# A two-model transformer kernel on one core: norm parts made with the residual, linears placed inside attentions, a position table stored from all partitions

## The reference

```python
def first_block(...):                     # DEPTH = 2
    for l in range(DEPTH):
        h = rms_norm(x, norm_mix[l])
        x = x + (even_mixer if l % 2 == 0 else odd_mixer)(h, ...)
        x = x + memory_cross_attention(rms_norm(x, norm_cross[l]), rms_norm(mem, norm_mem[l]), ...)
        x = x + conv_ffn(rms_norm(x, norm_ffn[l]), ffn_w_up[l], ...)
def second_block(...):
    for l in range(DEPTH):
        x = x + HALF_STEP * swiglu(rms_norm_2(x, ffn1_norm[l]), ...)
        x = x + hybrid_mixer(rms_norm_2(x, mix_norm[l]), positions, ...)
        x = x + memory_cross_attention_2(rms_norm_2(x, ca_norm[l]), rms_norm_2(mem, mem_norm[l]), ...)
        x = x + HALF_STEP * swiglu(rms_norm_2(x, ffn2_norm[l]), ...)
    return rms_norm_2(x, final_norm)
```

## Time and profile before

| | |
|---|---|
| median of 3 runs | 2695.26 us (2693.7 to 2696.86) |
| the profiled execution's own time | 2693.7 us |
| its span, first to last instruction | 2693.7 us |
| PE busy | 2426.5 us, 90% |
| weight loads busy | 2237.8 us, 83% |
| DVE busy | 1680.1 us, 62% |
| ACT busy | 1115.9 us, 41% |
| mean granted TensorE clock | 0.918 of 2.4 GHz |
| HBM read | 357.78 MB, 135 GB/s over the span |

### The profile page before, as it was taken

One profiled execution on the slowest core, in us unless ns is written; L12 is line 12 of the kernel. 1 busy time (PEld: TensorE's weight loads), 2 busy tenths in 40 slices (PEclk: granted clock), 3 DMA queues, 4 the chain that ended last, 5 costly groups with the idle time before them and its releaser, 6 DMA issues.

```text
span 2693.7 us, 40616 instructions
## 1 busy us (share of the span) xinstructions
PE 2426.5 (90%) x17557; PEld 2237.8 (83%) x17557; DVE 1680.1 (62%) x2336; ACT 1115.9 (41%) x1314; POOL 31.5 (1%) x53
## 2 busy tenths in 40 slices
PE   6877899997688998999998789999999998789998
PEld 6747799994578998999984578999999994578997
DVE  4465587755467877666446767666666445767664
ACT  4334454433355444334342354334334253345332
POOL 0103000000000000000000000000000000000000
PEclk8878999997799999999996789999999997789998
DMA  7525245450124554555540234554555640043552
GB/s 217 142 26 143 94 158 187 158 189 16 63 94 143 188 188 141 188 181 156 158 136 1 68 126 140 186 176 164 179 188 158 168 149 16 28 160 109 179 188 79
DMA packets 322821, 365.40 MB, mean 136 GB/s; under 512 B 24495, under 2 KB 298691, under 8 KB 322515
## 3 DMA queue, kind: packets, MB, share of 16 engines
q1 hardware_dynamic: 316723, 349.12, 39.8%
q0 software_dynamic: 4336, 7.31, 1.7%
q10 hardware_dynamic: 1584, 6.36, 0.6%
HBM read 357.78 MB, written 4.98 MB: 135 GB/s over the span
## 4 chain that ended last, share of the span: by engine, by line
PE 76%; DVE 14%; ACT 8%; issue 2%; DVEq 0%; DMA 0%; ACTq 0%; PEldq 0%
PE bank L630 22%; PE bank L633 21%; PE bank L631 21%; DVE wlo L1223 3%; PE bank L781 2%; PE bank L828 2%; ACT xs_hi L989 2%; DVE wk L1296 2%; ACT whi L937 2%; PE bank L717 1%; PE bank L817 1%; ACT wk L991 1%; PE bank L705 1%; PE bank L783 1%; PE bank L725 1%
## 5 line engine op out<-in xcount | busy, mean ns | idle before, releaser
L630 PE MATMUL bank<-xs_hi,wlo 128*128 128x256 f32 x3920 | 1013.5, 293 | 94.9 <-DVE xs_lo L1293 42.8
L631 PE MATMUL bank<-xs_lo,whi 128*128 128x256 f32 x3920 | 994.8, 289 | 0.0
L937 ACT ACTIVATE whi<-raw 128x2048 fp32r<-128x2048 f32 (+2 forms) x344 | 638.7, 1860 | 836.9 <-PE bank L633 814.5
L1223 DVE TENSOR_TENSOR wlo<-raw,whi 128x2048 fp32r<-128x2048 f32 (+2 forms) x344 | 761.5, 2224 | 237.9 <-ACT whi L937 237.7
L630 PEld LDWEIGHTS bank<-xs_hi,wlo 128*128 128x128 f32 x3920 | 771.3, 197 | 116.6 <-issue 94.9
L631 PEld LDWEIGHTS bank<-xs_lo,whi 128*128 128x128 f32 x3920 | 775.9, 198 | 0.3
L633 PE MATMUL bank<-xs_hi,whi 128*128 128x256 f32 (+1 forms) x3920 | 572.3, 287 | 0.0
L633 PEld LDWEIGHTS bank<-xs_hi,whi 128*128 128x128 f32 (+1 forms) x3920 | 520.9, 196 | 4.3
L630 PE MATMUL bank<-act_hi,wlo 128*128 128x256 f32 x1056 | 276.4, 283 | 5.4 <-DVE wlo L1223 5.4
L631 PE MATMUL bank<-act_lo,whi 128*128 128x256 f32 x1056 | 276.3, 283 | 0.0
L633 PE MATMUL bank<-act_hi,whi 128*128 128x256 f32 x1056 | 212.9, 283 | 0.0
(11 more groups left out here) (205 smaller groups left out, 2057.9 us busy)
## 6 DMA issues: line engine op xcount, KB each, us to landing
raw<-in_ffn_w_gu SPq DMA_DIRECT2D x88, 1024.0 KB, 5.1
...
```

The lines of the kernel that those rows point to most:

```text
L630: eng.matmul(out, a[1], b[0], start=first and i == 0, stop=False, skip_group_check=True)
L631: eng.matmul(out, a[0], b[1], start=False, stop=False, skip_group_check=True)
L937: eng.activation(whi[i % SETS][:, 0:ch["n"]], raw[i % SLOTS][:, 0:ch["n"]], ACT.Copy).then_inc(S["weights_hi"], 1)
L1223: eng.tensor_tensor(wlo[i % SETS][:, 0:n], raw[i % SLOTS][:, 0:n], whi[i % SETS][:, 0:n].bitcast(F32), ALU.subtract)\
```

## The change

1. **Norm parts with the residual.** A linear or `ffn` that adds to `xT` now takes `then`, the next norm. As soon as a pair of tiles of `xT` is added, ACT makes its two `hi` tiles and its squares (`norm_pair`), DVE its two `lo` tiles (`norm_lo`). The parts go to one of two buffers `X`. The squares of a pair are summed by PE with two fp32 matmuls (`sum_pair`), 8 for a norm; the reduction on DVE is gone.
2. **No barrier to the next linear.** A stage with `join=True` has no drain and no wait; normed linears and `ffn` are such. Their first two units run in lockstep, pair by pair of tiles as these come (`as_it_comes`). Linears after a `split` take the parts tile by tile in the same way; the `split` stage is gone. Other stages keep the barrier.
3. **Linears inside attentions.** `enroll` puts units in a list, and `fill={slot: (emit, evacuate)}` of a `heads`, `index` or `attention` stage says at which step PE emits them and ACT and DVE split and evacuate. Moved: 8 units of the even mixer's input, 6 of the odd mixer's, the value units of all four cross attentions (2 each), the 12 gate units of each hybrid mixer, and the first half (4 half units of 24 matmuls each) of the output projections of the even and the odd mixer. Attention now has two score banks instead of four, and its own output banks; mLSTM and differential attention have one bank for transposes and one for outputs.
4. **Gates.** The tanh is done later (`flush`), often at the end of an attention; the scale by 0.5 is folded into what follows.
5. **Memory.** Both memories are transposed and normed once (in two stages of linears and at the end of one `heads` stage), stored to DRAM as four tensors `mem_in`, and loaded as a chunk by each cross attention. Its units are evacuated by ACT ("plain").
6. **Start and tables.** Gains of the first norm and chunk 0 are loaded first; x is normed at once, and memory, tables and parameters are handled after the first two units. POOL waits for no stage: `rpb` and `na_skew` go first. The T5 table is made as `t5_rows`, the same row on all 128 partitions, and stored in four DMAs of 512 KB.

```diff
-            def norm_input(nm):
-                for k in range(KT):
-                    eng.activation(xs[0][:, k, :], nm["src"][:, k, :], ACT.Identity, scale=cols[:, nm["gain"] + k:nm["gain"] + k + 1], bias=C("zero"))\
-                       .then_inc(S["xs_hi"], 1)
-                eng.activation(square, nm["src"][:, :, :], ACT.Square).then_inc(S["sq_ready"], 1)
+            def norm_pair(nm, p):
+                signal, value = nm["pairs"][p]
+                eng.wait_ge(S[signal], value)
+                two = xT[:, 2 * p:2 * p + 2, :]
...
+                for k in (2 * p, 2 * p + 1):
+                    eng.activation(X[nm["buf"]][0][:, k, :], xT[:, k, :], ACT.Identity, scale=cols[:, nm["gain"] + k:nm["gain"] + k + 1],
+                                   bias=C("zero")).then_inc(S["xs_hi"], 1)
+                if p < 3:
+                    eng.activation(squares[p].rearrange("p (k c) -> p k c", c=SEQ), two, ACT.Square).then_inc(S["sq_ready"], 1)
...
-            def enter(i):
-                if i:
-                    eng.wait_ge(S["act_stage"], i)
-                    eng.wait_ge(S["dve_stage"], i)
+            def enter(i, st):
+                if i and not st["join"]:
+                    eng.drain().then_inc(S["pe_stage"], 1)
+                    if st.get("after"):
+                        eng.wait_ge(S["att_done"], st["after"])
+                    fill(st, "pre")
+                    eng.wait_ge(S["act_stage"], st["bar"])
+                    eng.wait_ge(S["dve_stage"], st["bar"])
...
+            def sum_pair(nm, p):
+                eng.wait_ge(S["sq_ready"], 4 * nm["n"] + p + 1)
+                for i in range(2):
+                    m = eng.matmul(post_bank[1][:, 0:SEQ], C("add128"), squares[p][:, i * SEQ:(i + 1) * SEQ],
+                                   start=p == 0 and i == 0, stop=p == 3 and i == 1, skip_group_check=True)
...
+            def unit(u):
+                un = units_of[u]
+                emitted[0] = u + 1
+                arrived(un["chunk"])
+                bank_free(u)
+                for o, operands in un["mms"]:
+                    m = product(lin_bank[u % 2][:, o], operands, True, True)
+                m.then_inc(S["lin_ready"], 1)
+
+            def fill(st, slot):
+                if slot in st["fill"]:
+                    while emitted[0] < st["fill"][slot][0]:
+                        unit(emitted[0])
...
                 for i in range(len(units) + lag + 1):
                     if i < len(units):
                         scores(i)
+                    fill(st, i)
                     if 0 <= i - lag < len(units):
                         turn(i - lag)
...
+            def fill(st, slot):
+                if slot in st["fill"]:
+                    emit_end, evac_end = st["fill"][slot]
+                    split_upto(units_of[emit_end - 1]["chunk"] + 2)
+                    evac_upto(evac_end)
...
+            attention("softmax", [small_head(o, 0, 9, h, h * HD, h, bias=C3("causal"), row=h, top_k=True, causal=True) for h in range(6)],
+                      fill={0: (G[4], G[3]), 2: (G[5], G[4]), 4: (G[6], G[5]), 6: (G[7], G[6])}, tanh=G[5])
...
-            eng.dma_start(t5_skew.ap(), t5_vec.unsqueeze(1).to_broadcast([4, SEQ, 512])).then_inc(S["t5_stored"], 16)
+            for h in range(4):
+                eng.wait_ge(S["t5_rows_made"], h + 1)
+                eng.dma_start(t5_skew.ap()[h].rearrange("(p n) c -> p n c", n=2), t5_rows[:, h, :].unsqueeze(1).to_broadcast([P, 2, 512]))\
+                   .then_inc(S["t5_stored"], 16)
+            spill(0)
```

1121 lines of the change are left out of this document (691 added, 430 removed).

## The result

The changed kernel takes **2628.0 us** (median; 2626.3 to 2628.3) beside 2695.0 us before: a ratio of 0.9753, 95% interval 0.9738 to 0.9769. One more execution of it took 7835.6 us; it is left out of these figures, and no record says what it waited for. It is faster by 67 us, where 248 us were forecast, and lies 53 us above the upper end of the range. The profiled execution took 2627.7 us with a span of 2625.9.

A forecast was written before the change was run, and what follows sets the result against it. PE bounds the feed-forward layers; hand-offs between engines and the half clock bound heads and attentions. 2693.7 less 156 (linears inside attentions) less 93 (joints, start) gives 2445, with 1.6 to the median 2447 us; range 2345 to 2575.

The forecast's parts named there:

- the factor of 1.165: Heads and attentions with moved units: time over PE's 566 us of full-clock work, giving 659 us and a 156 us gain.
- a rival of its own in the prediction: Filled attentions keep a clock near 0.73, so PE needs 775 us there: 2561 us in all, chance 0.08.
- PE and DVE take turns at being late: Filled attentions, unit between scores and transposes (place 1): alternating lateness, priced within 1.165, giving 659 us.
- slower than before: Every filled unit: splits issued only after the head's waits, 9.95 us a unit, 2801 us in all, chance 0.03.
- DVE as the smaller engine: Heads and attentions with moved units: DVE holds 438 us against PE's 566, so PE is the larger.
- Joints: Outside the filled attentions: feed-forward layers, cross attentions' linears, outputs, hybrids, inputs, branches and start together save 93 us.
- the hybrid split and output leave 26: Hybrid split and output: 33.8 us falls to 26 with parts tile by tile, saving 16 us for two.
- Three pairs of products before it needs the last: Feed-forward layer's end: PE has 8.3 us of work before needing the last pair, about 3 us late; 1 us left.
- Start: Kernel's start: first product at about 17 us instead of 31.2, yet 1 us lost overall; bounds 10 gained, 10 lost.
- Table store: Position table stored from 128 partitions: some 25 us from about 45, in time for the even mixer, worth nothing.
- Its rival's price, 66 us: Store still takes 95.6 us, so an evacuation stalls the even mixer some 66 us: 2511 us, chance 0.03.
- The two rules: Throttled clock is the default and activity releases it; ScalarE and VectorE queues are in-order. Both weighed for filled attentions.

The follow-up runs named there:

- e10: Changed kernel with units inside heads, index and attentions running 6 of their 48 matmuls, results wrong: 2523.8 us, ratio 0.9364.
- e11: Changed kernel with only 64 of 2048 columns copied and subtracted for units inside heads, index and attentions, all matmuls kept: 2570.6 us, ratio 0.9539.
- e3: Changed kernel with VectorE adding a finished unit to the residual before splitting the chunk after the next, in linears making norm parts: 2619.8 us, ratio 0.9730.
- e2: Changed kernel with barriers back at all 18 stages that joined the one ahead, norm parts still made with the residual: 2707.8 us, ratio 1.0058.
- e9: Changed kernel with each of the four position-table rows stored from 4 partitions in place of 128: 2682.2 us, ratio 0.9965.
- e13: Changed kernel with ScalarE, in attentions, copying the next chunk's weights ahead of its copy of the turned probabilities: 2612.5 us, ratio 0.9700.
- e16: Changed kernel with four thrown-away matmuls ahead of the wait for probabilities in 52 attention slots without a unit: 2645.9 us, ratio 0.9819.
- e17: Thrown-away matmuls added to the changed kernel with half units, add ahead of split, other slots and early weight copy together: 2622.0 us, ratio 0.9731.

## Why the prediction was wrong

- **Direction and kind: right.** Faster, with the attentions as the place of the largest gain.
- **The step that failed is the factor of 1.165** on TensorE's 566 us "in full-clock time". It took the filled stages as running at full clock and put all loss into idle time, 93 us. Measured: 560 us of full-clock work (6 less than forecast), 125 us idle (32 more) and 89 us of half clock (forecast 0). 32 + 89 - 6 = 115 us, the miss in these stages. On the forecast's 566 us the factor should have been 774.4/566 = 1.37. Its source mixed two measures: 37.9/34.31 = 1.10 is length over busy time at a clock of .55, while the factor was put on full-clock time, by which that stage is 37.9/(34.31 x 0.55) = 2.0. The clock was a rival of its own in the prediction, with a chance of .08 and a clock of .73 for all of it; in truth both held at once, the clock at .81 to .87 in the odd and hybrid mixers, and engines that wait in turn. The reason against that rival, that units in linears run at full clock, did not carry over: after 6.8 us without a matmul at the start of the sparse attention, the first unit ran at half clock for most of its length (granted clock at half from 2196.7 to 2206.9), its matmuls 0.21 us apart and then 0.12:

```profile
2200.24 1.61 PE L968 MATMUL bank<-ft 64*128 64x128 f32 x4 [6.78 <-DVEq L1480]
...
2204.94 0.41 PE L727 MATMUL bank<-x_hi,wlo 128*128 128x256 f32 x1
2205.15 0.41 PE L728 MATMUL bank<-x_lo,whi 128*128 128x256 f32 x1
...
2207.01 0.28 PE L727 MATMUL bank<-x_hi,wlo 128*128 128x256 f32 x1
2207.13 0.28 PE L728 MATMUL bank<-x_lo,whi 128*128 128x256 f32 x1
```

- **"PE and DVE take turns at being late"** was named, at place 1, but priced within the factor. e10 and e11 show its size: some 70 us of added idle time with few matmuls, 58 us back with a thin split. The rival "slower than before" had the mechanism (a unit's splits issued only after the head's waits), and in the sparse attention a unit cost 22.9/3 = 7.6 us, near the 7.8 at which nothing would be left of the gain, though not that rival's 9.95.
- **DVE as the smaller engine** (438 forecast, 429 measured): right, and of no use. An engine with room to spare can still set the time if its work stands in another's chain.
- **Joints.** Outside those stages the prediction saves 93 us, the trace 27 (2693.7 - 815 = 1879 to 2625.9 - 774.4 = 1852). The miss of 66 by place: hybrid branch, output, query and keys 102.4 and 99.8 for some 84, 33 us; the feed-forward layers 12 (the two with convolution 201 and 202 for 194.5) and what stands between them and the attentions 8; the even and odd mixers' outputs to keys 46.3 and 44.6 where the stretches of before, 208.9 to 285.6 and 704.8 to 780.5, less the moved 23.0 and the forecast 11.3 give 42.4 and 41.4, 7 us; the start 4. The step that failed in the hybrids is "the hybrid split and output leave 26": in the second one it is 38.1 us from the branch's end to the query's first product, with waits of 3.97 and 5.12 us in it; query and keys, 25.8 us from there, came as forecast. "Three pairs of products before it needs the last" holds in a feed-forward layer, whose splits are all made by then (waits of 0.9 to 1.5 us), but not behind an output linear, where the last add stands behind the split of the chunk after the next (5.1 us, and half clock after it). e3 gives 4.3 us of this in each hybrid. The branch linears went from 32.3 us at .99 to 38.9 and 35.9 at about .9.
- **No barrier.** e2 gives 82 us for it, of the order of the 93 forecast; but against a kernel with early parts and barriers, not against before.
- **Start.** First product at 21.0 for 17, and 60.0 us to the end of the part where 100.9 less eight moved units leave 54.8: it cost 5 us for 1. The term was mis-sized, the bound of 10 held.
- **Table store.** In time and worth nothing by itself: right, landing in 8.2 us each for the 25 expected. Its rival's price, 66 us, measured as 57, but that is luck in part: priced was an evacuation that waits for the table, and the wait that ended last in e9 was for weight loads beside the slow store.
- **The two rules.** Moving one copy ahead of another on ScalarE alone gave 14 us (e13). The Trainium skill (TensorE: Matmul & The Clock Gate, spec table and the note on queue depths) has ScalarE and VectorE as strict FIFO, in-order queues; e13 agrees. The clock of the stick-breaking attention went from .75 to .95 by thrown-away matmuls (e16). The Trainium skill (TensorE: Matmul & The Clock Gate, Part 1) says that the throttled state is the default and activity releases it; e16 agrees, while e17, where the same matmuls left the mean at .92 for .91, shows little of it. The half clock was weighed and then left out of the sum, where it took 89 us.
